# Top-k routing with fewer vector instructions to unpack a candidate, and one token tile's norm moved ahead of the next tile's

## The reference

```python
h = h + jnp.einsum('bsm,md->bsd', mixed, w_out[layer])
xn = rms_norm(h, norm_ffn[layer])            # x * rsqrt(mean(x*x) + 1e-6) * g
q = jnp.einsum('bsd,dq->bsq', xn, w_q).reshape(b, s, 8, 2, 128)
scores = jnp.einsum('bshcq,ckq->bshck', q, sub_keys)
top_s, top_i = lax.top_k(scores, 16)
cand_s = top_s[..., 0, :, None] + top_s[..., 1, None, :]      # 16 x 16 pairs
cand_i = top_i[..., 0, :, None] * 128 + top_i[..., 1, None, :]
best_s, pos = lax.top_k(cand_s, 16)
expert = jnp.take_along_axis(cand_i, pos, axis=-1)
gate = jax.nn.softmax(best_s, axis=-1)
```

## Time and profile before

| | us |
|---|---|
| median of three runs (lowest, highest) | 1670.76 (1669.7, 1673.65) |
| the profiled execution | 1677.62 |
| its span, first to last instruction | 1675.4 |
| PE busy | 1625.1 (97%) |
| DVE busy | 1323.9 (79%) |
| ACT busy | 703.8 (42%) |
| POOL busy | 594.1 (35%) |

### The profile page before, as it was taken

One profiled execution on the slowest core, in us unless ns is written; L12 is line 12 of the kernel. 1 busy time (PEld: TensorE's weight loads), 2 busy tenths in 40 slices (PEclk: granted clock), 3 DMA queues, 4 the chain that ended last, 5 costly groups with the idle time before them and its releaser, 6 DMA issues.

```text
span 1675.4 us, 28110 instructions
## 1 busy us (share of the span) xinstructions
PE 1625.1 (97%) x10843; PEld 1440.7 (86%) x10843; DVE 1323.9 (79%) x2700; ACT 703.8 (42%) x1065; POOL 594.1 (35%) x400
## 2 busy tenths in 40 slices
PE   8999999999999997999999999999999999999997
PEld 7876579887889997999999999989989898788886
DVE  5657676883999998998836668888798889998777
ACT  4234542343333334888943333333333333333334
POOL 3100054103567751000012236556566565542110
PEclk9999999999999998999999999999999999999999
DMA  7331010132243452566498799999999999999994
GB/s 259 101 99 52 1 53 4 52 115 96 98 140 126 131 168 85 198 237 255 180 350 312 241 328 349 343 340 350 374 364 343 344 363 346 411 412 359 328 313 159
DMA packets 130724, 384.51 MB, mean 229 GB/s; under 512 B 12704, under 2 KB 53920, under 8 KB 129568
## 3 DMA queue, kind: packets, MB, share of 16 engines
q1 hardware_dynamic: 83216, 210.18, 35.7%
q0 software_dynamic: 37728, 159.40, 25.5%
q10 hardware_dynamic: 9648, 13.14, 2.2%
HBM read 340.73 MB, written 39.85 MB: 227 GB/s over the span
## 4 chain that ended last, share of the span: by engine, by line
PE 36%; DMA 10%; DVE 6%; POOL 4%; issue 3%; ACT 1%; SPq 0%; DVEq 0%; ACTq 0%
PE ps L192 11%; PE ps L193 10%; PE ps L194 10%; DMA u_selected<-in_u_rows,expert_index 8%; PE ps L2332 5%; POOL v_selected L2086 3%; POOL u_selected L2077 2%; DVE h L2234 1%; DMA mixed<-hidden_ahead 1%; DMA wq_raw<-in_u_t 1%; DVE dot_products L2221 1%; DVE v_lo L2267 1%; DVE a_lo L2270 1%; DVE hidden L2263 1%; DVE u_lo L2203 0%
## 5 line engine op out<-in xcount | busy, mean ns | idle before, releaser
L192 PE MATMUL ps<-v_hi,a_hi 128*128 128x512 f32 x768 | 299.8, 390 | 5.8 <-DVE a_lo L2270 5.5
L194 PE MATMUL ps<-v_hi,a_lo 128*128 128x512 f32 x768 | 298.8, 389 | 0.0
L193 PE MATMUL ps<-v_lo,a_hi 128*128 128x512 f32 x768 | 298.8, 389 | 0.0
L2086 POOL DMA_INDIRECT v_selected<-in_v,expert_index x128 | 186.9, 1460 | 280.6 <-DVE h L2234 262.8
L192 PE MATMUL ps<-xn_hi,u_hi 128*128 128x384 f32 (+1 forms) x768 | 262.0, 341 | 8.1 <-DVE xn_lo L1500 3.7
L194 PE MATMUL ps<-xn_hi,u_lo 128*128 128x384 f32 (+1 forms) x768 | 259.3, 338 | 0.0
L193 PE MATMUL ps<-xn_lo,u_hi 128*128 128x384 f32 (+1 forms) x768 | 259.2, 338 | 0.0
L2077 POOL DMA_INDIRECT u_selected<-in_u_rows,expert_index x128 | 176.7, 1380 | 153.1 <-DVE hidden_selected L2221 123.2
L2267 DVE TENSOR_TENSOR v_lo<-wout_raw,v_hi 128x1024 fp32r<-128x1024 f32 x128 | 156.3, 1221 | 64.8 <-ACT v_hi L2175 64.2
L2175 ACT ACTIVATE v_hi<-wout_raw 128x1024 fp32r<-128x1024 f32 x128 | 135.2, 1057 | 146.2 <-PE ps L194 143.5
L2221 DVE CUSTOM_DVE_ANT_0 dot_products<-u_selected,xn_tok 128x1024 bf16<-128x1024 f32 x128 | 154.3, 1219 | 45.1 <-DMA u_selected<-in_u_rows,expert_index 45.0
(11 more groups left out here) (333 smaller groups left out, 2975.0 us busy)
## 6 DMA issues: line engine op xcount, KB each, us to landing
wq_raw<-in_u_t SPq DMA_DIRECT2D x128, 512.0 KB
wout_raw<-in_v SPq DMA_DIRECT2D x128, 512.0 KB
gate_matrix<-gate_stage POOLq DMA_DIRECT2D x6, 4096.0 KB, 13.8
gates<-gate_matrix SPq DMA_DIRECT2D x32, 768.0 KB
win_raw<-in_win_t SPq DMA_DIRECT2D x25, 512.0 KB, 4.0
mixed<-hidden_ahead SPq DMA_DIRECT2D x64, 192.0 KB
wq_raw<-in_wq_t SPq DMA_DIRECT2D x16, 512.0 KB
hidden_ahead<-hidden_route ACTq DMA_DIRECT2D x34, 192.0 KB, 2.4
```

Source lines behind the costliest of these rows:

```text
L192: nc.tensor.matmul(out, w_hi, m_hi, start=first, stop=False)
L193: nc.tensor.matmul(out, w_hi, m_lo, start=False, stop=False)
L194: return nc.tensor.matmul(out, w_lo, m_hi, start=False, stop=last)
L2086: pool.indirect_dma_start(v_sel[:, k % GB, :], None, v_rows, bass.IndirectOffsetOnAxis(S.expert[:, k:k + 1], 0)).then_inc(s_vsel[k % GB], 16)
```

## The change

In `finish`, the last two of the four tiles are put in another order, on three engines. The transposes of tile 2 come six products earlier on PE, in the midst of tile 3's second bank; six instead of four `k` steps of `ahead` stand ahead of tile 3's transposes; tile 3's squares are summed in two halves on ACT and its two bank additions on DVE alternate with the two low parts of tile 2. A column more in `h_ss` takes the second half's sum.

In `route`, `mark` finds the column with a mask, `4 * (2 * (p < 16) + (p < 40)) + 3 * (p < 56)`, which is 15 under 16, 7 in 16 to 39, 3 in 40 to 55 and 0 beyond; the column is `p` and-ed with the mask, bit by bit. The keys of rows get a leading column of zeros, so that all steps between neighbours are one subtraction.

```diff
@@ finish, ACT
+            def square_half(d):
+                act.wait_ge(s_res, 2 * GT + d + 1)
+                w = slice(d * T, (d + 1) * T)
+                st.do(act.activation(sq[:, w], S.h[:, GT, w], ACT.Square, scale=D ** -0.5,
+                                     accum_out=ss[:, GT + d:GT + d + 1]), s_ss)
+
...
             square(2)
             root(2)
-            square(3)
-            high(2, 0)
+            square_half(0)
+            for half in range(2):
+                high(2, half)
+            square_half(1)
             root(3)
-            high(2, 1)
             for half in range(2):
                 high(3, half)
@@ finish, DVE
             def scale(t):
                 r = ss[:, t:t + 1]
-                dve.wait_ge(s_ss, t + 1)
-                st.do(v.tensor_scalar(r, r, 1.0 / D, RMS_EPS, ALU.mult, ALU.add))
+                if t < GT:
+                    dve.wait_ge(s_ss, t + 1)
+                    st.do(v.tensor_scalar(r, r, 1.0 / D, RMS_EPS, ALU.mult, ALU.add))
+                else:
+                    dve.wait_ge(s_ss, GT + 2)
+                    st.do(v.scalar_tensor_tensor(r, r, RMS_EPS, ss[:, t + 1:t + 2], ALU.add, ALU.add))
...
             scale(2)
-            add(3)
-            scale(3)
-            low(2)
-            low(3)
+            add_half(GT, 0)
+            low_half(2, 0)
+            add_half(GT, 1)
+            low_half(2, 1)
+            scale(GT)
+            low(GT)
@@ finish, PE
             for o in range(4, 8):
                 for k in KB:
                     from_rwkv(o, k)
+                    if o == 7 and k == 1:
+                        transposes(2)
                 if o < 6:
                     transposes(o - 4)
-            transposes(2)
             pe.wait_ge(s_qlo, 1)
-            ahead(range(KT // 2))
+            ahead(range(KT - 2))
             transposes(3)
-            ahead(range(KT // 2, KT))
+            ahead(range(KT - 2, KT))
@@ route, mark
                                     pos[:, :, pair, :].rearrange("p t h k -> p t (h k)")))
-                for i, low in enumerate((7, 3)):
-                    st.do(v.tensor_scalar(bits[:, i, :].rearrange("p (t x) -> p t x", t=TT),
-                                          pos[:, :, pair, :].rearrange("p t h k -> p t (h k)"), low, None,
-                                          ALU.bitwise_and))
-                for c in range(2):
-                    st.do(v.tensor_copy(keyf[:, c, :, :].rearrange("p (t h) k -> p t h k", t=TT),
-                                        topi[:, :, pair, c, :]))
+                for keys_of, c in ((row_keys[:, :, 1:], 0), (col_keys[:, :, :], 1)):
+                    st.do(v.tensor_copy(keys_of.rearrange("p (t h) k -> p t h k", t=TT), topi[:, :, pair, c, :]))
                 st.settle()
                 starts, p_ = bc(S.const("row_starts"), 1, TH * TOPK), bc(posf[:, 0, :], 2, TOPK)
                 st.do(v.tensor_tensor(wide[0][:, :, :], p_, starts, ALU.is_ge))
-                st.do(v.tensor_copy(delta[:, :, 0:1], keyf[:, 0, :, 0:1]))
-                st.do(v.tensor_tensor(delta[:, :, 1:TOPK], keyf[:, 0, :, 1:TOPK], keyf[:, 0, :, 0:TOPK - 1],
-                                      ALU.subtract), s_eq)
-                st.do(v.tensor_copy(posf[:, 1:3, :], bits[:, :, :]))
-                st.do(v.tensor_scalar(acc[:, 1, :], posf[:, 0, :], 16.0, None, ALU.is_lt))
+                st.do(v.tensor_tensor(delta[:, :, :], row_keys[:, :, 1:], row_keys[:, :, 0:TOPK], ALU.subtract), s_eq)
+                st.do(v.tensor_scalar(posf[:, 1, :], posf[:, 0, :], 16.0, 2.0, ALU.is_lt, ALU.mult))
+                st.do(v.tensor_scalar(posf[:, 2, :], posf[:, 0, :], 56.0, 3.0, ALU.is_lt, ALU.mult))
                 st.settle()
...
-                st.do(v.tensor_tensor(posf[:, 2, :], posf[:, 2, :], posf[:, 1, :], ALU.subtract))
...
-                st.do(v.tensor_tensor(acc[:, 0, :], posf[:, 1, :], acc[:, 0, :], ALU.add))
+                st.do(v.scalar_tensor_tensor(acc[:, 1, :], posf[:, 0, :], 40.0, posf[:, 1, :], ALU.is_lt, ALU.add))
                 st.settle()
+                st.do(v.scalar_tensor_tensor(bits[:, 0, :], acc[:, 1, :], 4.0, posf[:, 2, :], ALU.mult, ALU.add))
+                st.settle()
+                st.do(v.tensor_tensor(bits[:, 1, :].rearrange("p (t x) -> p t x", t=TT),
+                                      pos[:, :, pair, :].rearrange("p t h k -> p t (h k)"),
+                                      bits[:, 0, :].rearrange("p (t x) -> p t x", t=TT), ALU.bitwise_and))
+                st.settle()
+                st.do(v.tensor_copy(acc[:, 0, :], bits[:, 1, :]))
+                st.settle()
                 st.do(v.tensor_tensor(wide[1][:, :, :], bc(S.const("iota")[:, 0:TOPK], 1, TH * TOPK),
                                       bc(acc[:, 0, :], 2, TOPK), ALU.is_equal), s_eq)
@@ route, DVE, once at its start
+            st.do(v.memset(row_keys[:, :, 0:1], 0.0))
```

More of the change, by code:

```diff
@@ L1479, in _, with add_half @@
                 st.do(v.tensor_tensor(S.u_lo[:, n, :], S.wq_raw[:, n, :], S.u_hi[:, n, :].bitcast(F32), ALU.subtract), s_qlo)
+            def add_half(t, d):
+                dve.wait_ge(s_mm, 2 * t + d + 1)
+                st.do(v.tensor_tensor(S.h[:, t, d * T:(d + 1) * T], S.h[:, t, d * T:(d + 1) * T],
+                                      S.ps[:, 2 * t + d, :], ALU.add), s_res)
             def add(t):
                 for d in range(2):
-                    dve.wait_ge(s_mm, 2 * t + d + 1)
-                    st.do(v.tensor_tensor(S.h[:, t, d * T:(d + 1) * T], S.h[:, t, d * T:(d + 1) * T],
-                                          S.ps[:, 2 * t + d, :], ALU.add), s_res)
+                    add_half(t, d)
             def scale(t):
                 r = ss[:, t:t + 1]
-                dve.wait_ge(s_ss, t + 1)
-                st.do(v.tensor_scalar(r, r, 1.0 / D, RMS_EPS, ALU.mult, ALU.add))
+                if t < GT:
[4 more added lines that the diff above has]
+                    st.do(v.scalar_tensor_tensor(r, r, RMS_EPS, ss[:, t + 1:t + 2], ALU.add, ALU.add))
                 st.settle()
@@ L1494, in scale, with low_half @@
                 st.do(v.scalar_tensor_tensor(xs[:, t, :], S.h[:, t, :], r, S.xn_tok[:, :], ALU.mult, ALU.mult), s_sc)
+            def low_half(t, half):
+                dve.wait_ge(s_thi, 2 * t + half + 1)
+                x = S.xn_lo[:, 4 * half:4 * half + 4, t * P:(t + 1) * P]
+                st.do(v.tensor_tensor(x, tile_bank(t, half),
+                                      S.xn_hi[:, 4 * half:4 * half + 4, t * P:(t + 1) * P].bitcast(F32),
+                                      ALU.subtract), s_tlo)
             def low(t):
                 for half in range(2):
[L1498 to L1502, removed]
+                    low_half(t, half)
             dve.wait_ge(s_x, 16)
@@ L1635, in route @@
         acc = sb("pos_acc", [P, 2, TH * TOPK])
-        keyf = sb("key_table", [P, 2, TH, TOPK])
+        col_keys = sb("col_keys", [P, TH, TOPK])
+        row_keys = sb("row_keys", [P, TH, 1 + TOPK])
         delta = sb("row_steps", [P, TH, TOPK])
@@ L1668, in weigh @@
                 x = wide[w][:, :, :].rearrange("p (h k) b -> p h k b", k=TOPK)[:, rows]
-                st.do(pool.tensor_tensor(x, x, bc((delta[:, rows, :], keyf[:, 1, rows, :])[w], 2, TOPK), ALU.mult), s_mul)
+                st.do(pool.tensor_tensor(x, x, bc((delta[:, rows, :], col_keys[:, rows, :])[w], 2, TOPK), ALU.mult), s_mul)
             for n in range(SPLIT, NW):
@@ L1893, in _ @@
                                   bc(small[:, :], 2, TOPK), ALU.mult), s_keys)
-            for w, table in ((1, keyf[:, 1, :, :]), (0, delta[:, :, :])):
+            for w, table in ((1, col_keys[:, :, :]), (0, delta[:, :, :])):
                 x = wide[w][:, :, :].rearrange("p (h k) b -> p h k b", k=TOPK)
@@ L2466, in build @@
                 S.gate_tok = sr("gate_tok", [P, NSEL])
-                S.h_ss = sr("h_ss", [P, TT])
+                S.h_ss = sr("h_ss", [P, TT + 1])
                 finish(nc, S, dram)
```

8 lines of the change are left out of this document (removed).

## The result

| | before | after |
|---|---|---|
| median of four runs of each, us | 1671.79 | 1648.86 |
| lowest, highest | 1669.7, 1673.65 | 1647.45, 1652.34 |
| the profiled execution; its span | 1677.62; 1675.4 | 1652.34; 1650.2 |
| ratio of the runs, 95% interval | | 0.9877 (0.9862 to 0.9893) |

The changed kernel takes 1.2% less, some 21 us. The sign was right, the size was not.

A forecast was written before the change was run, and what follows sets the result against it. PE, busy 97% of the span, was taken as the bound, its routing waits set by DVE. Marks 10, clock 0.4 and output projection 4.7 made 15.1 us off 1670.8: 1655.7 us, range 1650.5 to 1664.5.

The forecast's parts named there:

- PE's waits are the currency: Whole kernel: PE is busy 97%, so time is won at its waits; three in routing, 11.5 us, come from DVE.
- The output projection, 4.7 us: End of the output projection: the new order lets routing start 4.9 us earlier, taken as 4.7; lower end 1.5.
- The price of the new forms: Marks on DVE: new comparison, bitwise and float-to-integer instructions priced as their neighbours, 0.29 us each.
- I take 10 us: Four marks in routing: DVE's tables come 10 us earlier, and all of it reaches PE.
- The walk: New mark order along POOL's old rows: 2.0 us saved in the first mark, about 4.5, 1.2, 3.3 in the others.
- my upper end of 19.6: Four marks: 24 small instructions gone at 0.82 us each, stalls spread evenly, would save 19.6 us.
- the second rival: Marks drift ahead of POOL's pieces and meet fewer, DVE leaves PE no wait: about 1653 us; chance 0.15.
- my 10.4: Routing: time won on PE, 10 us from the marks plus 0.4 from the clock.
- the ceiling at 11.5 + 0.8 + 1.5 = 13.8: Most PE could gain in routing: waits 11.5 us, clock at a transpose tile 0.8, clock behind the 2.4 us wait 1.5.
- The 0.4 that I had counted for the clock: PE at the end of routing: half of 0.8 us lost to lowered clock in one tile of 24 products.
- Twelve pieces: From 650 us to the end: PE waits 5.5 and 2.8 us in twelve pieces, expected unchanged.
- this rival, PE made late by the gathers: Expert block: new gather phase makes DVE late, PE's 8.3 us of waits triple, about 1675 us; chance 0.04.

The follow-up runs named there:

- e_delay_8: The changed kernel with eight 128x2048 reductions to scratch on DVE behind the last mark; 1661.5 us, ratio 0.9931 to the kernel before.
- e_norm: The kernel before with only the new `finish`, `route` left old; 1665.0 us, ratio 0.9962.
- e_marks: The kernel before with only the new `route`, `finish` left old; 1654.6 us, ratio 0.9901.
- e_pieces_later: The kernel before with POOL's pieces of weighing two tiles later (behind 14, 25, 36 instead of 12, 23, 34); 1651.0 us, ratio 0.9885.
- e_four_ahead: The changed kernel with four instead of six `ahead` steps before the fourth tile's transposes; 1649.7 us, ratio 0.9885 to the kernel before.

## Why the prediction was right and where it was wrong

- **PE's waits are the currency, and DVE's top-k chain sets them.** Right. All 11.5 us went, where I had expected 2 to 4 us of waiting for the tables to stay. ACT's wait for its `exp` went with them, and e_delay_8 shows the wait coming back where the table is late.
- **The output projection, 4.7 us (4.9 at full clock).** Right: 4.9 in the profile, 0.0038 in e_norm's ratio, which is 6.3 us of 1669.8 with an interval from 4.0 to 8.5. The waits were 0.17 us in place of my 0.4. The clock stayed up.
- **The price of the new forms, 0.29 us.** Right: float result written as integer (L1831) 0.292 in all four, the bitwise one 0.29 where POOL let it. The half rate that the Trainium skill (Vector Engine (DVE) Microarchitecture Reference, "7. Points that are easy to get wrong") gives for a scalar-tensor-tensor with two SBUF sources does not show in these rows.
- **"I take 10 us" for the marks.** This step failed: DVE's tables came over 20 us earlier, not 10. The walk was right for mark 0 (2.0 forecast, 2.4 measured), and I then added up the other three at their old phases. Saved there were 7.3, 4.5 and 5.1, not 4.5, 1.2 and 3.3, since a mark that starts earlier meets other work of POOL: four pieces fell into mark 1 and four into mark 2 before, and none does now. Mark 3 never had pieces; its 5.1 us come from POOL's low parts, met at other places. The marks gave 19.3 us. That this is near my upper end of 19.6 is chance: the upper end spread the stalls evenly over the steps, and they are not spread so (7.3 us in one mark, 2.4 in another). The sums of candidates gave 6.2 more, a term that I had at nothing, and 2.5 were lost behind the last mark. I had written the mechanism down as the second rival (drift ahead of the pieces), at 0.15, and it came true.
- **What PE gets.** That PE could give up no more than its waits and the clock was right, and it kept the error small: DVE's 23.1 us were over twice my 10, the time won 15.4 against my 10.4. I had the ceiling at 11.5 + 0.8 + 1.5 = 13.8. Nearer is: the waits of 11.4, and 3.6 of the clock. That is an estimate: the clock was at half rate in 614.9 to 618.4 and 632.0 to 642.3, PE was busy for 7.3 us of that with products and transposes, and half of it is lost. The 0.4 that I had counted for the clock looked at one tile only.
- **"Twelve pieces" behind 650 us.** A misreading: the earlier trace rows has six and two, so eight. After the change there are seven, with 6.2 us in place of 8.3, so this rival, PE made late by the gathers, did not come. Nothing in the sum hung on the count.
- **The rest.** The medians are 22.9 us apart, the ratio is worth 20.6, the two parts 20.3. What lies over that is scatter: from the end of routing to the end of the span it is 1024.2 us in the execution of before, 1020.4 in the one of after, and 1015.4 to 1018.6 in all other profiles, whatever they changed; e_norm, with nothing new behind `finish`, has 1017.8. The execution of before was the longest of these in that stretch.

The range failed at its lower end. It was built on the likeliest case plus a little, though the upper end of the marks' gain stood in the same text. The 20.3 us that the profiles show would have landed on its edge (1670.8 - 20.3 = 1650.5), so the range had nothing over for scatter if the second rival came true.

## What to carry to other kernels

Where two engines keep each other out, ask not only how much an instruction costs but where the other engine's bulk work falls: moving it by one or two places in its queue, behind the short dependent steps, did as much for the time here as rewriting them, and both together did no more than one. A chain of short settled steps under such a neighbour had a lever of four to five here (5.6 us of own time taken away gave 23.1, 4 us added cost 18.5), so one walk at the old phases gives the first term only. Then cap the gain by the waits of the engine that sets the end, and by what it does at the lower clock around them: what lies over the cap is slack, and tells how much more work the faster engine could take for nothing.

## What the runs showed of the hardware that was not expected

- The interplay of DVE and POOL repeats almost exactly: the rewritten mark 1 took 9.06 or 9.07 us in five different programs, routing 243.7 to 243.8 us in eight. The last mark varied most, 13.30 to 13.45 us in the same five.
- Around the same wait of 3.72 us PE's clock was at half rate for 6.8 us in the kernel before and in e_marks, but for 3.4 us in e_pieces_later (it fell 0.8 us ahead of the end of the wait in the kernel before, 1.1 us behind it in e_pieces_later), and the way from the third scale to routing was 15.61, 15.30 and 14.50 us: the same code differs by a microsecond by when the clock falls and rises. After the waits of 1.00 us in e_four_ahead and 1.23 in e_norm it did not fall.
